# A streaming encoder layer on one core: rotary halves on ScalarE, recurrence gates issued between the queries, and eight gate chunks in split precision

## The reference: what is computed

```python
z = x @ w_in                      # columns: rnn stream | q | k | v | rnn gate | attn gate
u  = causal_conv4(z.rnn)          # sum over 4 taps of xc[t+j] * conv_w[j], plus conv_b
gx = sigmoid(blockdiag(w_x) u + b_x);  ga = sigmoid(blockdiag(w_a) u + b_a)
a  = exp(-8 * ga * softplus(-a_param))
h  = scan(h = a*h + sqrt(1 - a*a) * gx * u)
q, k = rope(z.q), rope(z.k)       # t1*cos - t2*sin, t2*cos + t1*sin, in halves of 32 features
o  = banded_attention(q, k, v)    # 16 query heads, 2 key heads, a sink per head
m  = sigmoid(z.gate_rnn) * (h @ w_br_rnn) + sigmoid(z.gate_attn) * (o @ w_br_attn)
x  = layernorm(alpha*x + m @ w_out)
x  = layernorm(alpha*x + shared_expert(x) + sum_top8 gate_e * expert_e(x))   # 64 experts
```

## Time and profile before

| | us |
|---|---|
| median of 3 runs | 1671.67 (1670.87 to 1672.03) |
| the profiled execution, its own time | 1677.62 |
| its span, first to last instruction | 1675.7 |
| TensorE busy | 1619.1 (97%) |
| VectorE busy | 759.2 (45%) |
| ScalarE busy | 523.6 (31%) |
| mean granted TensorE clock | 0.987 of full |

### The profile page before, as it was taken

One profiled execution on the slowest core, in us unless ns is written; L12 is line 12 of the kernel. 1 busy time (PEld: TensorE's weight loads), 2 busy tenths in 40 slices (PEclk: granted clock), 3 DMA queues, 4 the chain that ended last, 5 costly groups with the idle time before them and its releaser, 6 DMA issues.

```text
span 1675.7 us, 25240 instructions
## 1 busy us (share of the span) xinstructions
PE 1619.1 (97%) x9384; PEld 1049.5 (63%) x9384; DVE 759.2 (45%) x1576; ACT 523.6 (31%) x1030; POOL 23.0 (1%) x38
## 2 busy tenths in 40 slices
PE   7999999999999999999898999999999999999996
PEld 6967897655555555555488779965555555555553
DVE  5866665423423423423468556652333333333335
ACT  3264434122222222222232544431322322322322
POOL 2000000000000000000010000000000000000000
PEclk9999999999999999999989999999999999999999
DMA  7743466299999999999347325554999999999980
GB/s 205 206 153 114 104 162 246 101 367 400 400 398 403 391 408 396 404 394 405 118 108 233 128 76 128 157 226 181 393 400 401 402 398 399 396 404 394 409 356 29
DMA packets 166644, 477.35 MB, mean 285 GB/s; under 512 B 43301, under 2 KB 99173, under 8 KB 133813
## 3 DMA queue, kind: packets, MB, share of 16 engines
q1 hardware_dynamic: 164816, 473.50, 75.3%
q0 software_dynamic: 1408, 2.85, 0.6%
q10 hardware_dynamic: 356, 0.13, 0.0%
HBM read 474.88 MB, written 1.57 MB: 284 GB/s over the span
## 4 chain that ended last, share of the span: by engine, by line
PE 90%; DVE 6%; issue 1%; ACT 1%; DMA 1%; SPq 0%; DVEq 0%; ACTq 0%
PE ps L830 26%; PE ps L850 14%; PE ps L544 10%; PE ps L871 5%; PE ps L872 4%; PE ps L815 4%; PE ps L557 4%; PE ps L559 4%; PE ps L558 4%; PE ps L816 4%; PE ps L818 2%; DVE tmp L1348 2%; PE ps L571 1%; PE ps L638 1%; PE ps L859 1%
## 5 line engine op out<-in xcount | busy, mean ns | idle before, releaser
L830 PE MATMUL ps<-experts,xg 128*64 128x512 f32 x2048 | 450.5, 593 | 2.8 <-ACT xg L1125 2.8
L830 PEld LDWEIGHTS ps<-experts,xg 128*64 128x64 f32 x2048 | 148.4, 137 | 292.9 <-issue 292.9
L850 PE MATMUL ps<-experts,hidT 128*64 128x512 f32 x1024 | 233.9, 599 | 1.8 <-ACT hidT L1139 1.8
L1576 DVE TENSOR_TENSOR hid<-ps,hid 128x256 f32<-128x256 f32 x64 | 27.2, 425 | 388.4 <-ACT hid L1133 388.4
L544 PE MATMUL ps<-xT,dense 128*128 128x288 f32 x736 | 189.8, 415 | 0.7 <-issue 0.7
L557 PE MATMUL ps<-parts 128*128 128x288 f32 x608 | 180.7, 297 | 0.0
L559 PE MATMUL ps<-parts,dense_lo 128*128 128x288 f32 x608 | 179.1, 295 | 0.0
L544 PEld LDWEIGHTS ps<-xT,dense 128*128 128x128 f32 x736 | 139.8, 193 | 40.1 <-issue 1.9
L1147 ACT ACTIVATE yh<-ps,gsl 128x512 fp32r<-128x512 f32 x128 | 87.9, 687 | 228.2 <-PE ps L850 228.2
L1588 DVE SCALAR_TENSOR_TENSOR yl<-ps,gsl,yh 128x512 fp32r<-128x512 f32 x128 | 96.1, 751 | 124.4 <-ACT yh L1147 124.4
L1125 ACT ACTIVATE xg<-ps,gperm_all 128x256 f32<-128x256 f32 x256 | 130.6, 561 | 63.3 <-PE ps L818 59.7
(11 more groups left out here) (260 smaller groups left out, 1927.1 us busy)
## 6 DMA issues: line engine op xcount, KB each, us to landing
experts<-in_w SPq DMA_DIRECT2D x384, 1024.0 KB, 9.6
dense<-in_w_in SPq DMA_DIRECT2D x26, 1024.0 KB, 5.8
dense<-in_w_in SPq DMA_DIRECT2D x32, 256.0 KB, 4.6
dense<-in_w_br_rnn SPq DMA_DIRECT2D x8, 1024.0 KB, 5.0
dense<-in_w_br_attn SPq DMA_DIRECT2D x16, 512.0 KB, 6.7
dense<-in_w_out SPq DMA_DIRECT2D x8, 1024.0 KB, 5.0
dense<-in_ws SPq DMA_DIRECT2D x6, 1024.0 KB, 5.3
tok<-in_x_prompt SPq DMA_DIRECT2D x1, 1024.0 KB, 5.7
```

The source lines that it names most:

```text
L830: last = mm(ps[e % 2 * CAP:(e % 2 + 1) * CAP, 2, :], xg[:, k, e * CAP:e * CAP + CAP], experts[:, e, 0:2, k * DE:k * DE + DE], start=k == 0 ...
L850: last = mm(ps[e % 2 * CAP:(e % 2 + 1) * CAP, 3 + b, :], hidT[:, m, e % 2 * CAP:(e % 2 + 1) * CAP], experts[:, e, 2, m * D + b * 512:m * D ...
```

## The change

Three edits.

**Order and banks.** The query chunks and the recurrence gates are issued in turn: query chunk c, then the pair of gate matmuls of block c. Items 10 to 33 of the bank count are now q, gate, gate, q, gate, gate (`z_q`, `z_lru`), all over 6 banks; before the gate chunks TensorE waits until both counts are free.

**Rotary and first tap.** ScalarE copies the four 32-partition halves, exchanged, from PSUM to `rot` (`turn_halves`; two buffers of `tmp`), and VectorE then does three operations of 128 partitions: product by `cos` out of PSUM, product of `rot` by `sin`, and a subtraction. `turn_halves` stands in ScalarE's order just ahead of the two sigmoids of the same block; two high parts move behind blocks 1 and 3. The first of the convolution's four taps, with its bias, goes from VectorE to ScalarE.

**Split gate chunks.** The four pieces of the attention gate are added to `SPLIT`, so gate chunks 8 to 15 are `over_parts`. Their high parts (and the first two of the branches) are made after pairs 0, 1, 3, 4, 6, 7, their low parts after pairs 1, 2, 4, 5, 7.

```diff
-Z_RNN, Z_K, Z_V, Z_Q, Z_LRU, Z_GATE, ... = 0, 8, 9, 10, 18, 34, ...
+Z_RNN, Z_K, Z_V, Z_QL, Z_GATE, ... = 0, 8, 9, 10, 34, ...
-SPLIT = list(range(D_IN + 1, D_KV)) + list(range(D_Q, D_G)) + list(range(D_BR, D_ROUTER))
+SPLIT = list(range(D_IN + 1, D_KV)) + list(range(D_Q, D_G)) + list(range(D_G + 4, D_ROUTER))
+HIGH_WITH = (0, 1, 3, 4, 6, 7)
+LOW_WITH = (1, 2, 4, 5, 7)
+def z_q(c):
+    return Z_QL + 3 * c
+def z_lru(c, j):
+    return Z_QL + 3 * c + 1 + j
 # TensorE
-                for c in range(KC):
-                    over_parts(L, bank_of(L, Z_Q + c), D_Q + c // 2, c % 2 * P, x_hi, x_lo).then_inc(z_ready[c % 2], 1)
                 pe.wait_ge(wax_in, (L + 1) * 64)
                 for c in range(KC):
+                    i = z_q(c)
+                    over_parts(L, bank_of(L, i), D_Q + c // 2, c % 2 * P, x_hi, x_lo).then_inc(z_ready[i % 2], 1)
                     pe.wait_ge(u_ready, L * KC + c + 1)
                     for j in range(2):
-                        bank = bank_of(L, Z_LRU + 2 * c + j)
-                        mm(bank[:, 0:U], wax[:, j, c, :], u_[:, c, :], start=True, stop=True).then_inc(z_ready[j], 1)
+                        i = z_lru(c, j)
+                        mm(bank_of(L, i)[:, 0:U], wax[:, j, c, :], u_[:, c, :], start=True, stop=True).then_inc(z_ready[i % 2], 1)
+                for b in range(2):
+                    pe.wait_ge(z_free[b], z_count(L, Z_GATE))
                 def gate_chunks(ms):
                     for m in ms:
+                        if m >= KC:
+                            over_parts(L, bank_of(L, Z_GATE + m), D_G + m // 2, m % 2 * P, x_hi, x_lo).then_inc(z_ready[m % 2], 1)
+                            continue
 # ScalarE
+                    act.wait_ge(xc_edges, L + 1)
+                    activation(u_[:, m, :], B1[:, m, 0:U], ACT.Identity, bias=prm_all[...], scale=prm_all[...]).then_inc(first_tap, 1)
...
+                def turn_halves(i, c):
+                    n = L * (KC + 1) + c + 1
+                    act.wait_ge(z_ready[i % 2], z_count(L, i) + 1)
+                    if n >= 2:
+                        act.wait_ge(q_ready, n - 1)
+                    for x in range(4):
+                        a, b = 32 * x, 32 * (x ^ 1)
+                        last = activation(rot[a:a + 32, c % 2, :], ps[b:b + 32, z_bank(i), 0:T], ACT.Copy)
+                    last.then_inc(rot_ready, 1)
...
-                    if c >= KC - 2:
-                        high_parts(L, F_BR + c - (KC - 2))
+                    if c in HIGH_WITH:
+                        high_parts(L, F_G + HIGH_WITH.index(c))
 # VectorE
-                    link(V.tensor_scalar(u_[:, c, :], B1[:, c, 0:U], w(0), ..., ALU.mult, ALU.add))
...
-                    V.tensor_tensor(dst, bank[:, 0:T], C["cos"], ALU.mult)
-                    for x in range(4):
-                        a, b = 32 * x, 32 * (x ^ 1)
-                        last = V.tensor_tensor(rot[a:a + 32, :], bank[b:b + 32, 0:T], C["sin"][b:b + 32, :], ALU.mult)
-                    last.then_inc(z_free[i % 2], 1)
-                    V.tensor_tensor(dst, dst, rot, ALU.add).then_inc(q_ready, 1)
-                    if c in (1, 2):
-                        low_parts(L, 4 + c)
+                    dve.wait_ge(rot_ready, n)
+                    V.tensor_tensor(dst, bank[:, 0:T], C["cos"], ALU.mult).then_inc(z_free[i % 2], 1)
+                    link(V.tensor_tensor(rot[:, c % 2, :], rot[:, c % 2, :], C["sin"], ALU.mult))
+                    V.tensor_tensor(dst, dst, rot[:, c % 2, :], ALU.subtract).then_inc(q_ready, 1)
+                    if c in (1, 3):
+                        low_parts(L, 5 + c // 2)
...
-                    if c == KC - 1:
-                        low_parts(L, F_BR)
+                    if c in LOW_WITH:
+                        low_parts(L, F_G + LOW_WITH.index(c))
```

## The result

| | before | after |
|---|---|---|
| median, us | 1671.85 (1670.87 to 1672.36, 4 runs) | 1652.88 (1652.49 to 1654.89, 4 runs) |
| ratio, 95% interval | | 0.989 (0.9873 to 0.9907) |
| the profiled execution, its own time | 1677.62 | 1652.71 |
| its span; mean granted clock | 1675.7; 0.987 | 1650.9; 0.992 |

The change gains 19.0 us.

The account below looks back on a forecast made before the run. TensorE was taken as the bound, except where its own rows show a gap. Layer 0's gain of 4.8 us and layer 1's 8.3 made 13.1, taken from 1671.67 to give 1658.6 us, range 1654 to 1667.5.

Parts of the forecast that it names:

- stage, to the sample scores: First query to sample scores: with queries and gates in turn, scores start at 91.6 instead of 98.62, 7.0 us less.
- of it kept in layer 0, with the clock: Layer 0 up to the sample softmax: 3.8 us kept behind the parameter chain, less 2.0 for a clock drop.
- kept in layer 1, with the clock: Layer 1, which has no parameter chain: all 7.0 us kept, less 1.7 for half a clock drop.
- split gate chunks: Attention, eight chunks a layer from 4.08 to 3.34 us: 5.9 us at most, half taken, 3.0 a layer.
- The clock of layer 0: Layer 0: TensorE's 3.3 us wait for the sample softmax may bring its own half-rate drop, counted as 2.0 us.
- The source of the stage's gain: Query and gate stage: issuing queries and gates in turn was taken to bring the 7.0 us.
- The blocks: One query chunk plus gate pair on TensorE: 3.23 + 0.11 + 1.00 = 4.34 us, eight of them 34.7.
- The tail: Behind the last query chunk: TensorE, done at 89.6, waits 2.0 us for the last rotary until 91.6.
- The experts: Two thirds of the span, not touched by the change; their stretch should keep its length.
- ScalarE becomes the bound: Query stage rival: bound above 0.71 us a turned copy, gain gone at 0.92, 1690 at 1.2; slower had 0.06.
- Weight loads bound the split chunks: Attention rival: 4.5 us a chunk instead of 4.08, 6.7 lost, 1671.3; within the 0.06 for no change.
- The clock: Rival: clock falls in both layers, 6.9 us instead of 3.7, split brings nothing, 1667.8; gains of 4 to 10 had 0.25.

Follow-up runs that it names:

- first_low_early: Kernel after with the high and low part of gate piece 4 made ahead of pair 1 instead of behind pairs 0 and 1; 1653.52 us, ratio 0.9880.
- order_back: Kernel after with all eight queries ahead of all gate matmuls again, keeping six banks and the rotary copies on ScalarE; 1648.72 us, ratio 0.9855.
- copies_doubled: Kernel after with ScalarE making each of a query's four turned copies twice, the first into a place not read; 1674.41 us, ratio 0.9999.
- queries_only: Kernel after with gate chunks 8 to 15 as float32 again, the other edits kept; 1665.30 us, ratio 0.9957.
- tap_back: Kernel after with the first tap of the convolution on VectorE again; 1654.38 us, ratio 0.9878.
- chain_early: Kernel after with layer 0's parameter chain moved from behind the last rotary to behind the rotary of blocks 0 and 4; 1652.56 us, ratio 0.9877.
- rotary_back: Kernel after with the rotary on VectorE alone as before, new order and six banks kept; 1656.02 us, ratio 0.9895.
- before_kept: Kernel before with only more unused matmuls: seven instead of six ahead of xT's first fill, seven instead of four ahead of its second; 1665.78 us, ratio 0.9946.
- split_only: Kernel before with only the split of gate chunks 8 to 15 added; 1661.06 us, ratio 0.9931.
- idle_filled: Kernel after with three unused matmuls in TensorE's 2.29 us idle ahead of the transposes of k, both layers; 1652.59 us, ratio 0.9871.

## Why the forecast was right in part, and where it was wrong

The sum was made for a gain of 13.1, the medians moved by 19.0. The terms below are read from the traces of before and after; the stage and what is kept of it are counted from the first query to the first pair output. The spans of the two traces differ by 24.8, more than the medians: 3.0 of it stem from the first fill of layer 0, 1.4 from the second fill, 0.9 from the experts and 0.3 each from ahead of the first query and from the end, all places that the change leaves alone.

| term, us | forecast | measured |
|---|---|---|
| stage, to the sample scores | 7.0 a layer | 7.4 in layer 0, 7.7 from the start |
| of it kept in layer 0, with the clock | 3.8 - 2.0 | 84.25 (54.91 to 139.16) to 80.54 = 3.7 |
| kept in layer 1, with the clock | 7.0 - 1.7 | 84.24 (884.15 to 968.39) to 78.50 (870.18 to 948.68) = 5.7 |
| split gate chunks | 3.0 a layer | 4.77 a layer |
| sum | 13.1 | 3.7 + 5.7 + 9.5 = 18.9 |

**The step that failed is the split gate chunks.** I wrote "I take half of the saving, 3.0 us a layer", from "late by 0.6 to 1 us in three or four of them". The mechanism was right, its count was not. A pair with one chunk now takes 158.48 - 152.41 = 6.07 us and took 164.61 - 157.85 = 6.76, so a chunk gains 0.69 (forecast 0.74), 5.5 for eight. Of that 0.6 is lost at pair 2 and 0.1 at a later one, and nothing elsewhere. VectorE is late behind one low part of five, that of pair 1, which begins only when the output of pair 0 is there (idle of 0.62 ahead of 136.33). It is the only one that stands between two pairs with one chunk each: the others come behind or ahead of a pair with two, whose 9.4 us give VectorE the time. I had put the same delay on pair after pair with one chunk, and not followed it from one to the next. It is 1.8 us a layer, 3.5 of the 5.9 that were missing. first_low_early shows the cause: with this low part moved, the wait is gone.

**The clock of layer 0** was the second: "that wait may bring one of its own: 2.0". There was none. The half rate behind the idle of 2.29 lasted 3.4 us, not 6.9, it lay under the scores and the two gate chunks, and the wait for the softmax was 1.15 in place of 3.3. The softmax was ready at 102.8, 1.2 us before my 104.05. Against this stands the 0.73 that I had not seen: ScalarE's exponentials of the decay come behind the chain as well, and the next gate chunk waits for a bank.

**Layer 1** was near: 5.3 forecast, 5.7 measured. That is partly luck, since the half rate there was 3.4 us in this trace and none in two others with the same idle. **The source of the stage's gain** is the third miss, which the total hides: I laid it to the order, and order_back has it without the order.

**The blocks**: 4.17 us in place of 4.34; I had added 0.11 for each change of format on the word of the first two starts of a chunk; but 24 records at 0.133 and four at 0.245 are 4.17 already, so over a block it costs nothing. The tail: 2.29 for 2.0, of which 0.2 since a turned copy is 0.41 and not 0.36. **The first tap**: 0, as said. **The experts**: unchanged but for 0.9 us (from the first product on the router's choice to the transposes of the normalisation 531.11 before and 530.25 after), as said.

**The rivals.** *ScalarE becomes the bound* was well posed, and copies_doubled shows one price, 0.82, at which it takes the whole gain. The Trainium skill (ScalarE: Activation LUTs, What ACT_TABLE_LOAD costs) gives 0.186 us and 0.833 ns a column, an estimate of 0.43 for 288 columns; the trace has 0.41, near it. *Weight loads bound the split chunks*: the Trainium skill (Perfetto Trace Analysis, Identifying the Most-Contended Engine) goes by the share of weight loads, and read as a bound on one chunk, as the forecast's rival read it, that gives 4.5 us; the trace has 3.4 from 154.0 to 157.4. So the summed loads of a chunk are not its time here. Over the whole span their share barely moved, from 63% to 64%. *The clock*: I weighed it for the stage, where it is steady. I didn't weigh it for the places that the change leaves alone, where it moved a single execution by 3 us.

What stays open: which of the six banks and the lighter VectorE shortens the stage by how much, since no run had two banks with the rotary on ScalarE; why three runs of queries_only were slow at an equal mean clock; and why the clock falls after the idle ahead of the first fill of some 1.1 us in some executions only.

## What to carry to other kernels

When filler work is made shorter, follow the engine that it covers from one round to the next, with what ends each of its idle times, rather than charge one delay to all rounds of a kind. Look for work that waits on few buffers before its order is changed: here the old order with six banks and the lighter rotary did as well, and was cheaper at the tail. And before a gain of a few us is read from a trace, compare the granted clock window by window in places that the edit does not touch; filling three waits of 1.1 to 2.8 us with matmuls without use was worth 7.9 us here, as much as the smaller part of the change (7.2).

## What was not expected of the hardware

The half rate came in stretches of 3.4 us and multiples of it: 3.4, 6.8, 10.2 or 13.6, in each trace of the table. An idle of 2.29 us ahead of the transposes of k was followed by 3.4 us in layer 0 of after, queries_only, first_low_early, tap_back and chain_early; with idles of 2.66 and 2.03 close together it was 6.8, and so it was behind the single idle of 2.14 of rotary_back. In layer 1 neither is steady: 3.4 or none behind the first, and behind the pair of idles 6.8 before, 3.4 in before_kept (2.49 and 2.03) and 10.2 in split_only (3.45 and 1.45). The idle of about 1.1 us ahead of the first fill was followed by 6.8 or by none, from one execution of a kernel to another, and with one more matmul of 0.86 us in it by none in any of the three traces.

idle_filled had 13.6 us at half rate around the second fill, twice that of the kernel after, but so had first_low_early and tap_back, where nothing was filled: the traces give no ground to say that an idle filled in one place lets the clock fall for longer in the next.
